# The last conv row of a fused trunk layer: its group norm moved from transposed statistics to streamed means inside a slice of the output projection

## The reference, cut to what matters

```python
h = rms_norm(x, g_pre_mix)
hc, bg, cg, q, k, v = split(h @ w_in, 6)                 # each 512 wide
y_conv = bg * causal_conv3(cg * hc, w_conv)              # 512 channels
y_attn = chunked_band_attention(q, k, v, rel_bias)       # 8 heads of 64
y = concat(group_rms_norm(y_conv, g_conv_out, 8),        # 8 groups of 64 channels
           group_rms_norm(y_attn, g_attn_out, 8))
y = y @ w_out
x = x + rms_norm(y, g_post_mix)
h = rms_norm(x, g_pre_ffn)
gate, up = split(h @ w_ffn_in, 2)                        # 2 x 2816
x = x + rms_norm((silu(gate) * up) @ w_ffn_out, g_post_ffn)
```

## Time and profile before

| What | Value |
|---|---|
| median of 3 runs | 1099.07 us (1098.83 to 1099.09) |
| the profiled execution, device time | 1098.96 us |
| its span in the trace | 1097.2 us |
| PE busy | 1085.2 us, 99% of the span |
| PEld busy | 900.9 us, 82% |
| DVE busy | 791.2 us, 72% |
| ACT busy | 471.6 us, 43% |
| POOL busy | 154.9 us, 14% |
| matmuls of the output projection (L1236) | 81.5 us in the 348 of the largest group |

### The profile page before, as it was taken

One profiled execution on the slowest core, in us unless ns is written; L12 is line 12 of the kernel. 1 busy time (PEld: TensorE's weight loads), 2 busy tenths in 40 slices (PEclk: granted clock), 3 DMA queues, 4 the chain that ended last, 5 costly groups with the idle time before them and its releaser, 6 DMA issues.

```text
span 1097.2 us, 15872 instructions
## 1 busy us (share of the span) xinstructions
PE 1085.2 (99%) x5569; PEld 900.9 (82%) x5569; DVE 791.2 (72%) x1244; ACT 471.6 (43%) x799; POOL 154.9 (14%) x256
## 2 busy tenths in 40 slices
PE   8999999999999999999999999999999999999997
PEld 7888888887888888888888888888888888888886
DVE  6878888656666766869787878778787787555584
ACT  6642243366667556633232332223232256444541
POOL 2400000001101222202102211221121110000030
PEclk9999999999999999999999999999999999999999
DMA  7332114460010633517436444643544699776631
GB/s 270 107 124 77 51 54 139 157 220 15 21 59 20 230 133 117 174 56 231 136 119 213 162 137 141 207 137 123 193 160 161 201 319 374 231 230 229 212 116 77
DMA packets 117335, 168.30 MB, mean 153 GB/s; under 512 B 7881, under 2 KB 73433, under 8 KB 117281
## 3 DMA queue, kind: packets, MB, share of 16 engines
q1 hardware_dynamic: 99648, 107.50, 30.6%
q0 software_dynamic: 16464, 55.89, 14.4%
q10 hardware_dynamic: 1168, 4.20, 1.0%
HBM read 121.65 MB, written 49.04 MB: 156 GB/s over the span
## 4 chain that ended last, share of the span: by engine, by line
PE 68%; DVE 1%; ACT 0%; issue 0%; POOL 0%; DVEq 0%; POOLq 0%
PE psum L1354 35%; PE psum L1381 19%; PE psum L1236 8%; PE psum L941 4%; PE psum L930 1%; PE psum L984 1%; PE psum L965 0%; PE psum L955 0%; PE psum L1073 0%; PE psum L1080 0%; DVE arena L2728 0%; ACT misc L1431 0%; DVE arena L2382 0%; DVE arena L2668 0%; PE psum L974 0%
## 5 line engine op out<-in xcount | busy, mean ns | idle before, releaser
L1354 PE MATMUL psum<-arena_r,ws 128*128 128x512 f32 x960 | 224.1, 389 | 0.0
L1354 PEld LDWEIGHTS psum<-arena_r,ws 128*128 128x128 f32 x960 | 180.2, 188 | 37.4
L1354 PE MATMUL psum<-hT,ws 128*128 128x512 f32 x720 | 169.9, 389 | 0.0
L1354 PEld LDWEIGHTS psum<-hT,ws 128*128 128x128 f32 x720 | 135.1, 188 | 28.0
L1381 PE MATMUL psum<-hT 128*128 128x512 f32 (+1 forms) x600 | 135.2, 385 | 0.0
L1381 PEld LDWEIGHTS psum<-hT 128*128 128x128 f32 x600 | 111.3, 188 | 22.5
L2537 DVE TENSOR_TENSOR misc<-misc,psum 128x512 f32<-128x512 f32 x100 | 68.4, 684 | 47.9 <-PE psum L1354 45.7
L941 PE MATMUL psum<-hT,ws 128*128 128x512 f32 (+1 forms) x432 | 95.7, 373 | 0.0
L1192 PE MATMUL psum<-arena_r,ws 128*128 128x512 f32 x372 | 86.9, 389 | 0.0
L941 PEld LDWEIGHTS psum<-hT,ws 128*128 128x128 f32 x432 | 72.6, 189 | 15.1 <-issue 2.2
L1827 ACT ACTIVATE ws<-o_raw 128x512 fp32r<-128x512 f32 x40 | 25.1, 628 | 138.9 <-DVE o_raw L2515 138.4
(11 more groups left out here) (273 smaller groups left out, 1567.6 us busy)
## 6 DMA issues: line engine op xcount, KB each, us to landing
raw<-in_w_ffn_in SPq DMA_DIRECT2D x44, 512.0 KB, 4.5
act_scratch<-arena POOLq DMA_DIRECT2D x77, 256.0 KB, 3.2
raw<-in_w_in SPq DMA_DIRECT2D x22, 512.0 KB, 4.0
arena<-in_w_ffn_out POOLq DMA_DIRECT2D x22, 512.0 KB, 5.5
arena<-act_scratch SPq DMA_DIRECT2D x38, 256.0 KB, 3.4
arena<-in_x SPq DMA_DIRECT2D x16, 512.0 KB, 5.9
raw<-in_w_out SPq DMA_DIRECT2D x16, 512.0 KB, 3.5
raw<-act_scratch SPq DMA_DIRECT2D x26, 256.0 KB, 3.3
```

The lines of the kernel that those rows point to most:

```text
L1354: last = mm(blocks(bank), w[:, k * P:(k + 1) * P], b_operand(i, part, k), start=fresh_bank and k == 0 and w is hi and part == 0, stop=k == ...
```

## The change

The last conv row is normed in the way of the other three. Its rounded squares go to arena row 10 (`SQ_HIGH`) and their low part to row 11 (`SQ_LOW`). A second copy of the 1/64 matrix is made in `misc` (`same_head_last`). The four matmuls of the means run inside slice 2. ACT takes the reciprocal root at its step 2. DVE makes the Newton step and the final multiplication at its step 2, ahead of `o_scale`. The transposes of the last attention output go from inside slice 3 to inside slice 4, and `attn_last` from DVE's step 3 to its step 4. The small matmuls, the power on POOL, the spreading on ACT, the eight transposes and their semaphores go.

```diff
@@ PE
-            def conv_stats(bank):
-                pe.wait_ge(consts_made, 5)
-                for i in range(NT):
-                    last = mm(bank[:, 2 * i:2 * i + 2], row(CU, P, i * P), group[:, :], start=True, stop=True)
-            def conv_norms(bank, first, n):
-                for b in range(n):
-                    last = tr(bank[:, b * P:(b + 1) * P], row(CR, P, (first + b) * P), ident[:, :])
+            def means(bank, heads, high, low):
+                for half in range(2):
+                    for part in (high, low):
+                        last = mm(bank[:, half * HALF:(half + 1) * HALF], heads, row_r(part)[:, half * HALF:(half + 1) * HALF],
+                                  start=(part == high), stop=(part == low))
+                last.then_inc(conv_stat, 1)
             def transpose_last_o():
-                pe.wait_ge(conv_var, 1)
+                pe.wait_ge(mix_done, 1)
                 transpose_o(PAIRS, PP[3])
+            def last_means():
+                for half in range(2):
+                    pe.wait_ge(half_free[half], OUT0)
+                pe.wait_ge(tile_free, PAIRS * NT + 1)
+                pe.wait_ge(conv_mixed, means_split(LAST))
+                means(PP[3], same_head_last, SQ_HIGH, SQ_LOW)
-            INSIDE = {3: transpose_last_o, 10: rows_inside(0), ...}
+            INSIDE = {2: last_means, 4: transpose_last_o, 10: rows_inside(0), ...}
-                if c == 2:
-                    ... conv_stats(PP[3]).then_inc(conv_stat, 1)
-                if c == 6:
-                    pe.wait_ge(oT_read, PAIRS)
-                    pe.wait_ge(conv_rs, 1)
-                    conv_norms(PP[3], 0, NT).then_inc(conv_norm, 1)
@@ ACT, behind the last attention step
-            square_conv(LAST), square_pair(LAST)
+            square_conv(LAST)
+            act.wait_ge(o_psum, PAIRS * NT)
+            spread_heads(same_head_last)
+            act.wait_ge(conv_sq, squared(LAST, 0))
+            go(row_r(SQ_HIGH), row(CU), ACT.Copy).then_inc(conv_sq, 1)
+            square_pair(LAST)
@@ ACT, loop over slices
-                if c == 4:
-                    act.wait_ge(oT_psum, PAIRS)
-                    spread_conv()
+                if c == 2:
+                    act.wait_ge(conv_stat, PAIRS)
+                    go(row(SQ_HIGH), PP[3], ACT.Abs_reciprocal_sqrt, bias=eps_col[:, 0:1]).then_inc(conv_root, 1)
@@ DVE
+            def mix_row(t, mean, f, out, done):
+                dve.wait_ge(conv_root, t + 1)
+                chain(stt(mean, mean, EPS, f, ALU.add, ALU.mult))
+                chain(stt(mean, mean, -0.5, f, ALU.mult, ALU.mult))
+                chain(stt(f, mean, 1.5, f, ALU.add, ALU.mult))
+                stt(out, row(CONV_ROWS[t]), params[:, t, 3:4], f, ALU.mult, ALU.mult).then_inc(done, 1)
                     split_out_w(2), split_out_a(2)
+                    low_sq(LAST, SQ_HIGH, SQ_LOW)
                     sum_squares(PAIRS)
-            def conv_last_stats():
-                dve.wait_ge(conv_stat, PAIRS)
-                ts(var[:, :], PP[3][:, 0:16], 1.0 / HD, EPS, ALU.mult, ALU.add).then_inc(conv_var, 1)
             def conv_last(_):
-                dve.wait_ge(conv_norm, 1)
-                stt(row(PAIRS - 1), PP[3], params[:, LAST, 3:4], row(CV), ALU.mult, ALU.mult).then_inc(mix_done, 1)
+                mix_row(LAST, PP[3], row(SQ_HIGH), row(PAIRS - 1), mix_done)
                 dve.wait_ge(mix_done, 1)
-            tasks = {3: [(attn_last, 0)], 5: [(conv_last, 0)],
+            tasks = {4: [(attn_last, 0)],
                 if c == 2:
-                    conv_last_stats()
+                    conv_last(0)
                     o_scale(PAIRS)
```

More of the change, by code:

```diff
@@ L259, in trunk_layer @@
         same_head = misc_r[:, 3 * 512:3 * 512 + P]
+        same_head_last = misc_r[:, 2304:2304 + P]
+        SQ_HIGH, SQ_LOW = 10, 11
         s1, s2 = [o_raw[:, 4 * n:4 * n + 4, :].rearrange("p i c -> p (i c)") for n in range(2)]
@@ L421, in trunk_layer @@
         conv_sq = sem("conv_sq")
-        conv_factors = sem("conv_factors")
-        conv_rs = sem("conv_rs")
         conv_stat = sem("conv_stat")
-        conv_var = sem("conv_var")
         o_var = sem("o_var")
@@ L429, in trunk_layer @@
         pool_seq = sem("pool_seq")
-        conv_norm = sem("conv_norm")
         conv_root = sem("conv_root")
@@ L804, in _ @@
                            ).then_inc(ext_stored, 16)
-            def conv_norm_factors(t):
-                pool.wait_ge(conv_var, 1)
-                factors_to(crs[:, :], var[:, :], 16, conv_factors, 1)
             def o_norm_factors(t):
@@ L830, in _ @@
                 o_norm_factors(t)
-            conv_norm_factors(PAIRS - 1)
             def norm_factor(i, sums, factors, done, value):
@@ L1074, in transpose_o @@
                 last.then_inc(oT_psum, 1)
-            def conv_stats(bank):
-                pe.wait_ge(consts_made, 5)
-                for i in range(NT):
-                    last = mm(bank[:, 2 * i:2 * i + 2], row(CU, P, i * P), group[:, :], start=True, stop=True)
-                return last
-            def conv_norms(bank, first, n):
-                for b in range(n):
-                    last = tr(bank[:, b * P:(b + 1) * P], row(CR, P, (first + b) * P), ident[:, :])
-                return last
             def values(i, steps, part):
@@ L1201, in stats @@
                     pe.wait_ge(conv_mixed, mixed(t - 1))
[L1202 to L1206, removed]
+                means(PP[2], same_head, CR, CU)
             behind = {(4, 2): 0, (5, 1): 1, (5, 5): 2}
@@ L1268, in _ @@
             BEFORE = {12: 1, 21: 4, 23: 5}
-            INSIDE = {3: transpose_last_o, 10: rows_inside(0), 13: rows_inside(2), 19: rows_inside(3)}
+            INSIDE = {2: last_means, 4: transpose_last_o, 10: rows_inside(0), 13: rows_inside(2), 19: rows_inside(3)}
             for c in range(len(PASSES) * KT):
@@ L1543, in square_y, with spread_heads @@
                 go(row(CU), row(CONV_ROWS[t]), ACT.Square).then_inc(conv_sq, 1)
+            def spread_heads(to):
+                go(to.rearrange("p (g d) -> p g d", d=HD),
+                   group[:, :].rearrange("p (g o) -> p g o", o=1).broadcast_to([P, 2, HD]), ACT.Copy, scale=1.0 / HD)
             def high_sq(t):
@@ L1549, in high_sq @@
                     act.wait_ge(consts_made, 6)
-                    go(same_head.rearrange("p (g d) -> p g d", d=HD),
-                       group[:, :].rearrange("p (g o) -> p g o", o=1).broadcast_to([P, 2, HD]), ACT.Copy, scale=1.0 / HD)
+                    spread_heads(same_head)
                 if t > 0:
@@ L1559, in conv_roots @@
                 go(row(CR), bank, ACT.Abs_reciprocal_sqrt, bias=eps_col[:, 0:1]).then_inc(conv_root, 1)
[L1561 to L1566, removed]
             scale = -HD ** -0.5
@@ L2100, in tap, with low_sq @@
                     chain(stt(v[:, n:SEQ], u[:, 0:SEQ - n], w, v[:, n:SEQ], ALU.mult, ALU.add))
-            def low_sq(t):
+            def low_sq(t, high=CR, low=CU):
                 dve.wait_ge(conv_sq, squared(t, 1))
-                tt(row_r(CU), row(CU), row_r(CR).bitcast(F32), ALU.subtract).then_inc(conv_mixed, 1)
-            def mix_row(t):
-                f, mean, y = row(CR), PP[2], row(CONV_ROWS[t])
+                tt(row_r(low), row(CU), row_r(high).bitcast(F32), ALU.subtract).then_inc(conv_mixed, 1)
+            def mix_row(t, mean, f, out, done):
                 dve.wait_ge(conv_root, t + 1)
@@ L2112, in mix_row, with mix_front @@
                 chain(stt(f, mean, 1.5, f, ALU.add, ALU.mult))
-                stt(y, y, params[:, t, 3:4], f, ALU.mult, ALU.mult).then_inc(conv_mixed, 1)
+                stt(out, row(CONV_ROWS[t]), params[:, t, 3:4], f, ALU.mult, ALU.mult).then_inc(done, 1)
+            def mix_front(t):
+                mix_row(t, PP[2], row(CR), row(CONV_ROWS[t]), conv_mixed)
             def gated_round(n):
@@ L2176, in _ @@
             make_u3(4)
-            mix_row(0)
+            mix_front(0)
             dve.wait_ge(prod, multiplied(4, 3))
@@ L2193, in _ @@
                 if n == 5:
-                    mix_row(1)
+                    mix_front(1)
                 make_u3(n)
@@ L2210, in _ @@
                 if n == 5:
-                    mix_row(2)
+                    mix_front(2)
                 front_low(n + 1, 4), front_low(n + 1, 5)
```

## The result

The changed kernel takes 1103.38 us (median of 6 runs, 1103.16 to 1104.30) against 1099.01 before (6 runs, 1098.83 to 1099.16). The ratio is 1.0042, with a 95% interval of 1.0032 to 1.0052: slower, by 4.4 us. The forecast was 1101.9 in a range of 1100.6 to 1104.5. Four of the six took 1103.16 to 1103.44 us, the other two 1104.02 and 1104.30. The profiled execution took 1103.16 us, 4.20 more than that of before.

The account below looks back on a forecast made before the run. TensorE was taken to bound the kernel from 361 us on. Saving 1.6 us and losing 4.4 to a stall makes it 2.8 later: 1101.75 on the profiled 1098.96, 1101.9 with the median's 0.11; range 1100.6 to 1104.5.

Parts of the forecast that it names:

- TensorE's work: Output projection: 2.50 us of small matmuls and factor transposes go, 0.90 of means come; gain 1.60 if TensorE never waits.
- The means in time: Slice 2: squares, matrix and DVE's added low part (1.14 us) fit in DVE's 2.30 us of idle time, costed at nothing.
- The root: ACT's step 2: table load 368.60 to 369.88, root to 371.00, DVE starting the Newton step at 371.1.
- drain behind a table load: ACT's table switch also costs 1.38 us of drain: stall 5.8 us, time 1103.3; a rival with chance 0.04.
- The chain on DVE: DVE's step 2: four dependent instructions, 371.1 to 376.18, ahead of slice 4's split, which ends 379.83, 6.2 us later than before.
- stall of 4.4: Ahead of slice 4: TensorE could come at 375.56 but starts at 379.94, waiting 4.4 us for DVE's split.
- No second stall and nothing given back: Behind slice 4: weights for slice 6 arrive with 1.8 us margin; everything from slice 6 on stays 2.8 us later.
- The clock: TensorE's granted clock around the wait ahead of slice 4: forecast to stay at full speed, costing nothing.
- stall of 4.4, clock stays: The main forecast: TensorE waits 4.4 us ahead of slice 4 at full clock; 1101.3 to 1102.4 us, chance 0.64.
- rival 1: The clock falls to half in the stall ahead of slice 4, costing 1.7 to 3.0 us, middle 2.3: 1104.2 us; chance 0.18.
- the tail's 4.6 us: Kernel's end: granted clock falls about 4.6 us after the last matmul, slightly longer than the forecast stall; cited against a fall.

Follow-up runs that it names:

- a_spread: Changed kernel with DVE's Newton instructions spread around and behind slice 4's split, attention scaling first, attention transposes back in slice 3: 1097.05 us, ratio to before 0.9983.
- b_split_first: Changed kernel with the whole Newton step and final multiplication at DVE's step 3, behind slice 4's split; run twice: medians 1101.28 and 1100.78 us.
- e_no_newton: Changed kernel without the three Newton instructions on the last conv row, using ACT's root as given: 1097.98 us, ratio to before 0.9990.
- c_busy_pe: Changed kernel with 12 more 128x512 matmuls inside slice 3, repeating its first tile's products in TensorE's idle time: 1101.89 us, ratio to before 1.0026.
- f_no_table: Changed kernel with a plain copy, needing no table load, for the last conv row's reciprocal root; three times: 1102.28 us (6 runs), then 1100.51 and 1102.37.

## Why the prediction was right or wrong

- TensorE's work. Right, a little too small. Forecast: 2.50 go, 0.90 come. The means took 0.91. a_spread, which has the saving without a wait, gained 2.0 us by its median and not 1.60. In the chain, from the start of the 24 matmuls at 361 to the transposes of slice 10, it takes 41.28 us where before took 43.16, 1.88 less. Most of the rest over 1.60 lies in the 128x512 matmuls themselves: the same 174 of them take 39.73 us in the chain of before and 39.49 in that of a_spread. Of these 0.24, 0.17 is in the 24 behind the small statistics matmuls (5.62, where 24 at the 0.227 of a_spread's block of 126 are 5.45). Why those are slower no run shows.
- The means in time: right. DVE's low part stood in its idle time (1.18 us of 2.30 are left), and slice 2 ran on.
- The root. Right. Table load and root came as worked out, to 0.05 us beside the execution's 0.19 offset. The Trainium skill's drain behind a table load (ScalarE: Activation LUTs, "What ACT_TABLE_LOAD costs") is not in this trace: the root starts 1.30 us after the load does.
- The chain on DVE. Forecast 371.1 to 376.18 and slice 4's split done at 379.83; measured 370.87 to 375.94 and 379.60. The stall of 4.4 was 4.38. Place, cause and size hold, and a_spread, b_split_first and e_no_newton each move the time with them.
- No second stall and nothing given back: right. PE touches from 379.74 on.
- The clock. This is the step that failed. The sum put the clock at nothing ("stall of 4.4, clock stays", chance 0.64, 1101.3 to 1102.4), and the measured 1103.38 lies above that; what happened is rival 1, which had 0.18. By the times it fell in every run of the changed kernel (lowest 1103.16, where c_busy_pe without the fall has 1101.66). The argument against it was weak: that the shorter waits of before left the clock alone says nothing on a wait that is longer than all of them, and the tail's 4.6 us is one fall, not the shortest time that one needs. The rival's price of 2.3 was too high: measured 1.70, half of the 3.4 us that the stretch lasted, where I had allowed up to 6. That price was drawn from the first blocks of the kernel; their pitch is double, but the granted clock reads 1.00 in the windows there, so no row ties them to the lower level.
- The range held the time because it was drawn over rival 1, and not because the forecast's sum came out. Without the slow stretch the sum was right: c_busy_pe gives its 1101.9.

Left open: why two of eight executions of f_no_table, and two of six of the changed kernel (1104.02 and 1104.30), take another 0.7 to 1.2 us. The mean granted clock on record is lower in them (0.995 in three, 0.997 in the fourth, against 0.997 to 0.998 in the executions one level below), so more time at the lower clock goes with it. Where it lies no trace shows. What decides between fall and no fall at the same wait is open too.

## What to carry to other kernels

Where TensorE bounds a stretch, work saved on it is only worth something if what it waits for next is ready sooner too; before moving an engine's work forward, list what stands behind it in that engine's order and the time by which each is due. A chain of dependent full-width instructions ahead of an operand split costs whatever goes beyond the slack of that split; put one between two splits at a time, and let the first free the buffer that others wait for. A wait of TensorE as long as the shortest that was followed by the low clock here (2.56 us) is to be counted as the wait plus a slow restart of about 1.7 us, and for one of 4.38 us or more, after which every execution here shows it, that is the forecast and not a rival.

## What the runs showed of the hardware

The granted clock is at one of two levels, 2.4 and 1.2 GHz, and whether a wait of TensorE brings the lower one depends on more than its length. After waits of 0.59 and 1.66 us no execution shows a fall by its time; after 2.56 us 11 of 20 do, after 3.27 us 6 of 8, after 4.38 us 6 of 6, after 8.17 us 4 of 4. The fall can come behind the restart (380.0 for a restart at 379.74, 380.3 for one at 378.86) or in the idle time (2.1 us after the last matmul). The cost in the traces was 1.59 to 2.05 us, and so the same kernel has two times, by the medians of b_split_first 1.34 us apart. The Trainium skill (TensorE: Matmul & The Clock Gate, "The HAM clock gate") has the fall come from idle time, seen through a free-running window. The two profiles of b_split_first, one wait with the fall and without, agree with a dependence on where the wait falls, but no run here shows what decides.
